# Router query loads of a two-layer encoder trunk, split by rows into pieces of unequal size

## The reference

```python
def peer(xn, wq, k1, k2, u, v):
    q = (xn @ wq).reshape(B, S, PEER_HEADS, 2, PEER_HALF)      # 8 heads, 2 sides of 128
    s1 = jnp.einsum('bshd,nd->bshn', q[..., 0, :], k1)         # 128 keys a side
    s2 = jnp.einsum('bshd,nd->bshn', q[..., 1, :], k2)
    t1, i1 = lax.top_k(s1, 16)
    t2, i2 = lax.top_k(s2, 16)
    ...                                                        # top 16 of the 256 pairs: idx, gate
    act = jax.nn.gelu(jnp.einsum('td,ted->te', x_blk, u[i_blk]))
    return jnp.einsum('te,ted->td', g_blk * act, v[i_blk])     # blocks of 128 tokens
```

## Time and profile before

| | us |
|---|---|
| median of three runs | 3361.7 |
| the profiled execution | 3362.57 |
| its span | 3360.5 |
| TensorE matmuls busy | 2869.8 (85%) |
| VectorE busy | 1985.9 (59%) |
| GpSimd busy | 726.9 (22%) |
| ScalarE busy | 582.6 (17%) |
| mean DMA rate over the span | 366 GB/s |

### The profile page before, as it was taken

How to read it: one execution, slowest core, us unless ns; L and a number is a source line. 1 busy time by engine, 2 the same in 40 slices (tenths; PEclk the granted TensorE clock), 3 DMA queues, 4 the chain that set the end, 5 groups by cost and what they waited for, 6 DMA issues and landing times.

```text
span 3360.5 us, 25410 instructions
## 1 busy us (share of the span) xinstructions
PE 2869.8 (85%) x8488; PEld 1577.6 (47%) x8488; DVE 1985.9 (59%) x3817; ACT 582.6 (17%) x1269; POOL 726.9 (22%) x563
## 2 busy tenths in 40 slices
PE   6999998888897877777789999888889787777777
PEld 5877864444443333333338786444444333333333
DVE  3444555565666666566666755556566666666565
ACT  3344411111110101010114541111111110101011
POOL 0000013322322222222210002332223222222221
PEclk9999999999999999999999999999999999999999
DMA  5544589999999999999995448999999999999998
GB/s 207 164 163 149 188 334 427 427 427 426 426 427 424 425 426 427 424 407 427 419 399 179 138 138 340 428 426 427 427 422 423 427 423 427 424 423 428 414 427 350
DMA packets 138464, 1229.48 MB, mean 366 GB/s; under 512 B 12897, under 2 KB 13665, under 8 KB 67553
## 3 DMA queue, kind: packets, MB, share of 16 engines
q0 software_dynamic: 73728, 1073.77, 75.5%
q1 hardware_dynamic: 63888, 148.67, 12.6%
q10 hardware_dynamic: 720, 5.44, 0.4%
HBM read 1225.74 MB, written 2.10 MB: 365 GB/s over the span
## 4 chain that ended last, share of the span: by engine, by line
PE 50%; DMA 38%; DVE 7%; ACT 2%; issue 2%; POOL 0%; DVEq 0%; SPq 0%; ACTq 0%; POOLq 0%
DMA ring_sb<-in_peer_uv_dram,idx_cur 36%; PE bank L1164 26%; PE bank L896 15%; PE bank L948 5%; DVE ring_sb L1637 5%; PE bank L960 1%; ACT diag L722 1%; DVE w_parts L386 0%; PE bank L1112 0%; ACT shared L718 0%; PE bank L983 0%; PE bank L1148 0%; ACT w_parts L380 0%; DMA ring_sb<-in_mlstm_w_out_dram 0%; DVE shared L1650 0%
## 5 line engine op out<-in xcount | busy, mean ns | idle before, releaser
L1164 PE MATMUL bank<-ring_sb,diag 128*128 128x512 f32 x4096 | 1946.8, 631 | 437.4 <-ACT diag L722 437.2
L1637 DVE CUSTOM_DVE_ANT_0 ring_sb<-ring_sb,arena 128x2048 f32<-128x2048 f32 x512 | 1172.5, 2291 | 841.7 <-DMA ring_sb<-in_peer_uv_dram,idx_cur 841.6
L1164 PEld LDWEIGHTS bank<-ring_sb,diag 128*128 128x128 f32 x4096 | 805.6, 201 | 1537.6 <-issue 924.0
L533 POOL DMA_INDIRECT ring_sb<-in_peer_uv_dram,idx_cur x512 | 696.8, 1361 | 1858.3 <-PE bank L1164 1844.6
L896 PE MATMUL bank<-w_parts,actT_hi 128*128 128x512 f32 x1664 | 523.4, 396 | 14.5 <-DVE w_parts L386 9.9
L718 ACT ACTIVATE shared<-shared 128x2 f32<-128x2 f32 (+1 forms) x272 | 55.8, 205 | 2145.4 <-DVE shared L1646 2145.4
L386 DVE TENSOR_TENSOR w_parts<-ring_sb,w_parts 128x2048 fp32r<-128x2048 f32 x100 | 228.3, 2290 | 210.4 <-ACT w_parts L380 210.4
L896 PEld LDWEIGHTS bank<-w_parts,actT_hi 128*128 128x128 f32 x1664 | 313.2, 190 | 82.7 <-issue 14.6
L896 PE MATMUL bank<-w_parts,actT_lo 128*128 128x512 f32 x832 | 326.8, 393 | 0.0
L380 ACT CAST w_parts<-ring_sb 128x2048 fp32r<-128x2048 f32 x100 | 190.8, 1911 | 303.7 <-DMA ring_sb<-in_mlstm_w_in_dram 160.5
L722 ACT ACTIVATE diag<-const,shared 128x128 f32<-128x128 f32 x512 | 179.5, 395 | 89.7 <-DVE shared L1650 89.1
(11 more groups left out here) (168 smaller groups left out, 1086.0 us busy)
## 6 DMA issues: line engine op xcount, KB each, us to landing
ring_sb<-in_mlstm_w_in_dram SPq DMA_DIRECT2D x48, 1024.0 KB, 5.2
ring_sb<-in_attn_w_in_dram SPq DMA_DIRECT2D x20, 1024.0 KB, 5.2
ring_sb<-in_mlstm_w_out_dram SPq DMA_DIRECT2D x16, 1024.0 KB, 5.1
arena<-in_peer_wq_dram SPq DMA_DIRECT2D x16, 1024.0 KB, 15.8
ring_sb<-in_attn_w_out_dram SPq DMA_DIRECT2D x16, 1024.0 KB, 5.1
wq_more<-in_peer_wq_dram SPq DMA_DIRECT2D x12, 1024.0 KB, 12.0
ring_sb<-in_peer_uv_dram,idx_cur POOLq DMA_INDIRECT x512
ring_sb<-in_peer_wq_dram SPq DMA_DIRECT2D x4, 1024.0 KB, 7.5
```

The lines of the kernel that those rows point to most:

```text
L533: nc.gpsimd.indirect_dma_start(out=uv_slot[at], out_offset=None, in_=uv_rows, in_offset=bass.IndirectOffsetOnAxis(ap=idx_cur[par][:, k:k + ...
L1164: last = mm(acc[n][:, :], diag[slot_of(gu, k)][:, :], v_slot[at][:, n * CH:(n + 1) * CH], start=False, stop=end and k == TOPK - 1, skip_gr ...
L1637: v.tensor_tensor_reduce(u_slot[at], u_slot[at], xn[b], 1.0, 0.0, ALU.mult, ALU.add, dots[:, k:k + 1]).then_inc(dot_done, 1)
```

## The change

Of each layer, the loads of heads 3 to 7 are no longer single DMAs of 128 rows. A table gives for each head and half the numbers of rows of its pieces; heads 0, 1 and 2 aren't in it and stay whole. The pieces go in order over the rows of the same source and destination, and raise the same semaphore, each by 16. TensorE's wait counts the pieces of all earlier loads of that buffer instead of the loads. In all, ten loads a layer become 29 DMAs, with the same bytes.

```diff
+        QUERY_ROWS = {(3, 0): (120, 8), (3, 1): (120, 4, 4), (4, 0): (112, 14, 2), (4, 1): (112, 13, 3),
+                      (5, 0): (112, 12, 4), (5, 1): (112, 11, 5), (6, 0): (112, 10, 6), (6, 1): (112, 9, 7),
+                      (7, 0): (120, 7, 1), (7, 1): (120, 5, 3)}
+
+        def query_rows(h, half):
+
+            return QUERY_ROWS.get((h, half), (P,))
+
+        def queries_landed(l, h, half):
+
+            earlier = [(m, i) for i in range(l + 1) for m in range(1, HEADS) if m % 2 == h % 2 and (i < l or m <= h)]
+            return 16 * sum(len(query_rows(m, half)) for m, _ in earlier)
...
                 def load(h, slots, landed):
                     for i in range(2):
-                        sp.dma_start(slots[i].rearrange("p k n -> p (k n)"),
-                                     rows[bass.ds(h * P + l * HEADS * P, P), i * SLOT:(i + 1) * SLOT]).then_inc(landed[i], 16)
+                        at = 0
+                        for n in query_rows(h, i):
+                            first = (l * HEADS + h) * P + at
+                            sp.dma_start(slots[i][at:at + n].rearrange("p k n -> p (k n)"),
+                                         rows[first:first + n, i * SLOT:(i + 1) * SLOT]).then_inc(landed[i], 16)
+                            at += n
...
                 slots, landed = (wq_odd, wq_odd_landed) if h % 2 else (wq_even, wq_even_landed)
-                loads = l * (HEADS // 2) + (h + 1) // 2 if h % 2 else l * (HEADS // 2 - 1) + h // 2
                 for side, half in parts:
                     if side == 0:
-                        pe.wait_ge(landed[half], 16 * loads)
+                        pe.wait_ge(landed[half], queries_landed(l, h, half))
```

## The result

The changed kernel takes 3458.6 us (median of five runs, 3453.7 to 3460.7) against 3361.3 us before: ratio 1.0283, 95% interval 1.0269 to 1.0297. It is 97 us slower, where 10 us faster was forecast. The profiled execution took 3458.8 us with a span of 3456.8.

The account below looks back on a forecast made before the run. The prediction took full DMA engines in the gathers, one of them late, to bound the kernel: 3362.57 - 10.0 gain + 0.4 for pieces = 3353.0, and with the median 0.9 lower 3352 us, range 3346 to 3365.

Parts of the forecast that it names:

- What bounds the kernel: In both layers' gathers, full DMA engines at 427 GB/s set the time; one engine ends about 6.5 us late.
- How the pieces are dealt: Each piece's rows go in equal shares to the most engines up to 16 dividing them, starting from the first.
- The cost of the pieces: 19 more DMAs a layer cost only completion packets: 0.2 us a layer, 0.4 in all.
- the window with two small loads: Window 799.5 to 820, with two 64 KB loads: 425 against 427 GB/s, read as 0.1 us for two small DMAs.
- other dealing: Rival on the cut loads: 120 rows might take only 8 engines, +4 to +17 us; 0.05 together with overhead.
- The rule against the change: Skill's rule against partition splits and small DMAs: 38 pieces at 2 us in series, +76 us, 3438; chance 1 in 50.
- The late engine is 15: Chosen, not read: the late engine in the gathers is 15, which the change relieves of 11.7 us a layer.
- the counts in the prediction: A layer's rows of the 29 pieces by engine, from 93 on engine 0 to 42 on engine 15, against 80 before.
- one of the first: Rival: the late engine is among the first seven and gets more rows; up to 3370 us; chance 0.10.
- The gain, limited by the lead,: Relieved engine can lead the last by 6.5 us at most, so each layer's gathers end 5.0 us earlier, -10.0 in all.
- Uneven dealing and overhead: Rival on the cut loads: pieces dealt otherwise than assumed, or overhead, make the kernel slower; chance 0.05.
- not dealt as assumed: Rival: 120 rows on only 8 engines, +4 to +17 us, or rows spread evenly, no change; small chance each.

Follow-up runs that it names:

- e12_one_row: Against the kernel before: loads of heads 3 to 7 leave out all but one row of each half, 10 rows a layer; 3321.1 us, ratio 0.9876.
- e1_columns: Against the kernel before: the same ten loads a layer cut into 29 DMAs by columns, each with all 128 rows; 3363.7 us, ratio 1.0006.
- e5_own: Against the kernel before: rows 64 to 127 of heads 3 to 7 left out, the rest in eight-row pieces stepped by four rows; 3366.3 us, ratio 1.0013.
- e9_own_dest: Against e5_own: only the destination is stepped by four partitions, source rows are eight in a row; 3365.7 us, ratio 1.0012.
- e6_cross: Against e5_own: same bytes, number and size of DMAs, but each piece is eight rows in a row on both sides; 3454.8 us, ratio 1.0279.
- e11_only0: Against e5_own: pieces of one row, meant to leave these loads on engine 0 only, other rows left out; 3353.9 us, ratio 0.9976.
- e14_0to1: Against e5_own: pieces of two rows, meant to leave these loads on engines 0 and 1 only, other rows left out; 3356.1 us, ratio 0.9979.
- e15_0to2: Against e5_own: pieces of three rows, meant to leave these loads on engines 0 to 2 only, other rows left out; 3354.4 us, ratio 0.9981.
- e10_no4to7: Against e5_own: pieces of four rows, meant to leave these loads on engines 0 to 3 only, other rows left out; 3368.9 us, ratio 1.0028.
- e2_112_16: Against the kernel before: all ten loads a layer cut into 112 and 16 rows, eight rows on every engine; 3433.5 us, ratio 1.0215.
- e8_early: Against the kernel before: only the loads of heads 1 and 2, before the first gather, cut into 112 and 16 rows; 3361.0 us, ratio 0.9997.
- e7_no7: Against e5_own: pieces of seven rows, meant to leave these loads on engines 0 to 6 only, other rows left out; 3367.7 us, ratio 1.0017.

## Why the prediction was wrong

- **What bounds the kernel** was right: DMA work in the gathers' stretches decides (e12_one_row), one engine is late there, and the tail with one engine of sixteen is there before and after.
- **How the pieces are dealt** held as far as it was seen: the 248 packets are what it gives. That the shares start from the first engine, no run shows directly.
- **A small misreading:** TensorE's digits in the long stretches are not all 7 and 8; each stretch has a 9. Nothing hangs on it.
- **The cost of the pieces is the step that failed.** It stood at 0.2 us a layer, for completions alone, because rows were counted by engine at 0.307 us each wherever they go. No term asked where an engine writes. The kernel measures 48.7 us a layer (97.4 / 2), of which the number of pieces is about 1 (e1_columns: 2.0 in both layers, within the noise). In its place stands: when the engines of a load write other partitions than with 128 rows, busy engines move less, the pieces (16.2 instead of 26.0 GB/s an engine in head 5's window) and the gathers beside them (18.1 instead of 26.5). The row that hinted at nothing was the window with two small loads; those have all 128 rows, like e1_columns' pieces. It was no neighbour of the pieces, and I took it as one. The range's upper bounds for other dealing, +17 us, had the same gap.
- **The rule against the change**, weighed at 1 in 50, had the sign and nearly the size (+76 us) by a reason that the runs refute: the 2 us for each DMA aren't paid (e1_columns, e5_own). What the Trainium skill says of the swizzle, as told above from "DMA: Bandwidth & Descriptors", would have given a reason to ask: it gives the engines' partitions for transfers to 128. e5_own and e9_own_dest against e6_cross agree with it for the first eight engines.
- **The late engine is 15** was a choice, and wrong by e5_own, where engine 15 is relieved of all these rows and nothing is gained. The step in the table points to engine 3, to which the change gives nine rows a layer more by the counts in the prediction, 2.8 us. That is the rival "one of the first", and accounts for some 6 us of the 97 at most.
- **The gain, limited by the lead,** was right in kind: relieved of 24.6 us a layer, the late engine brought 3 to 4 us a layer against the kernel before (e11_only0, e14_0to1, e15_0to2, all with 140 further DMAs) and 7 against e10_no4to7; 5.0 was the forecast for 11.7 us. That the sizes are near is partly luck, as the engine was another. In the changed kernel no gain is seen.
- **Rivals.** Uneven dealing and overhead were held at 0.05 together; the "not dealt as assumed" one is refuted by the packets as to the number of engines. e2_112_16 leaves little of the loss to unevenness, e1_columns little to overhead. The case that came true wasn't among them.

What stays open is the size of the loss. Per row that crosses, if rows are dealt in order, 112 and 16 costs 71.8 / 2260 = 0.032 us, 120 and 8 102.4 / 2320 = 0.044, the changed kernel 97.4 / 2296 = 0.042, 64 and 64 87.1 / 1280 = 0.068, and e6_cross 93.1 / 1120 = 0.083. So the number of crossing rows alone doesn't set it. It is dearer where many engines meet at few places: sixteen engines at the lower 64 partitions, eight at eight partitions. That fits, as do the 242 GB/s of the pieces alone in e8_early, but it was not tested by itself. The Trainium skill ("SBUF — State Buffer", door 1) gives each such place as a port of SBUF; that the ports are what is short is argued here. Shown is only that the destination partitions decide. No version here that loads all rows beats the kernel before; the faster ones leave rows out.

## What to carry to other kernels

Work shared by sixteen DMA engines isn't a heap that can be dealt again at will: in this kernel, beside a full stream, loads of all 128 partitions cost no more when cut by columns, and 72 to 102 us more when cut by rows. So keep further loads on all 128 partitions where you can, and if one must be cut, try it by columns first. When a DMA share stays full and GB/s falls, look for transfers that write each other's places, not for idle time. And before work is taken off an engine, find out by experiment which engine is late, and how far it can run ahead of the others: the gain ends there.

## What was unexpected of the hardware

- Busy DMA engines moved 289 GB/s instead of 426 for 21 us around loads of 2 MB in pieces; the time lost by one cut head is 11.2 us, over twice the 4.9 us that the whole load takes alone at 427 GB/s.
- Pieces of 112 and 16 rows are slow with nothing beside them: 242 GB/s on full engines instead of 426 in the same window (e8_early).
- Further DMAs are cheap on full queues: 38 more for 2 us (e1_columns), and 140 more, with rows left out, for 4.6 to 7.6 us (e5_own, e7_no7, e10_no4to7).
- One engine is late by about 6.5 us at the ends of the gathers, and by the step above it is likely engine 3, not one of the last. That it has queue 14's instruction fetches, at 0.97 us each, is the prediction's reading of one gap between tiles; no run tests it.
